# Products with 0/1 tables as two passes of high and low parts, in the forget gates and the stick-breaking attention of a two-block transformer kernel

## What is computed

```python
def stick_breaking_attention(q, k, v):           # per block of 128 queries
    z = jnp.einsum("bqhd,bshd->bhqs", qb, k) * scale
    earlier = kpos[None, :] < qpos[:, None]
    log_keep = jnp.where(earlier, jax.nn.log_sigmoid(-z), 0.0)
    log_after = lax.cumsum(log_keep, axis=3, reverse=True) - log_keep
    w = jnp.where(earlier, jnp.exp(jax.nn.log_sigmoid(z) + log_after), 0.0)
    return jnp.einsum("bhqs,bshd->bqhd", w, v)

def forgetting_attention(q, k, v, log_f):
    cum = jnp.cumsum(log_f, axis=1)
    z = jnp.einsum("bqhd,bshd->bhqs", qb, k) * scale + cq[..., None] - cum[:, :, None, :]
    p = masked_softmax(z, kpos[None, :] <= qpos[:, None])
    return jnp.einsum("bhqs,bshd->bqhd", p, v)
```

## Time and profile before

| | |
|---|---|
| median of three runs | 1865.68 us |
| the profiled execution | 1863.92 us, of it span 1861.9 us |
| TensorE products | 1841.9 us busy, 99% of the span, 9402 |
| VectorE | 1032.0 us, 55% |
| ScalarE | 876.5 us, 47% |
| GpSimd | 153.4 us, 8% |
| mean granted TensorE clock | 0.999 |

### The profile page before, as it was taken

One profiled execution on the slowest core, in us unless ns is written; L12 is line 12 of the kernel. 1 busy time (PEld: TensorE's weight loads), 2 busy tenths in 40 slices (PEclk: granted clock), 3 DMA queues, 4 the chain that ended last, 5 costly groups with the idle time before them and its releaser, 6 DMA issues.

```text
span 1861.9 us, 22247 instructions
## 1 busy us (share of the span) xinstructions
PE 1841.9 (99%) x9402; PEld 1576.7 (85%) x9402; DVE 1032.0 (55%) x997; ACT 876.5 (47%) x1076; POOL 153.4 (8%) x169
## 2 busy tenths in 40 slices
PE   8999999999999999999999999999999999999998
PEld 6889988898888998889888888888888888888886
DVE  5665544564755655447475655555455545545544
ACT  6454543564645454346363444454353444435443
POOL 1300011000240001100020000010000101100011
PEclk9999999999999999999999999999999999999999
DMA  8866555455577555545555645554546555455553
GB/s 274 239 184 205 172 169 169 128 193 192 169 215 216 168 171 192 169 137 183 192 198 187 203 159 191 180 177 166 190 156 221 178 168 180 155 165 197 181 181 113
DMA packets 187154, 338.96 MB, mean 182 GB/s; under 512 B 6848, under 2 KB 48688, under 8 KB 186160
## 3 DMA queue, kind: packets, MB, share of 16 engines
q1 hardware_dynamic: 181536, 316.89, 52.0%
q0 software_dynamic: 5232, 20.59, 4.0%
q10 hardware_dynamic: 288, 0.07, 0.0%
HBM read 335.43 MB, written 2.10 MB: 181 GB/s over the span
## 4 chain that ended last, share of the span: by engine, by line
PE 94%; DVE 2%; ACT 2%; issue 1%; DMA 0%; ACTq 0%; DVEq 0%
PE acc L1540 27%; PE acc L1542 27%; PE acc L1541 27%; PE bank L1693 3%; PE bank L1633 1%; DVE w_lo L1004 1%; PE bank L1682 1%; PE bank L1662 1%; ACT w_hi L658 1%; PE bank L1623 1%; PE bank L1801 1%; PE acc L1589 0%; PE bank L1651 0%; PE bank L1652 0%; PE bank L1650 0%
## 5 line engine op out<-in xcount | busy, mean ns | idle before, releaser
L1004 DVE TENSOR_TENSOR w_lo<-raw,w_hi 128x2048 fp32r<-128x2048 f32 (+4 forms) x308 | 675.6, 2197 | 572.9 <-ACT w_hi L658 572.7
L1540 PE MATMUL acc<-w_hi,xt_hi 128*128 128x512 f32 (+4 forms) x2400 | 909.4, 379 | 0.5 <-DVE w_lo L1004 0.3
L1542 PE MATMUL acc<-w_hi,xt_lo 128*128 128x512 f32 (+4 forms) x2400 | 902.3, 376 | 0.0
L1541 PE MATMUL acc<-w_lo,xt_hi 128*128 128x512 f32 (+4 forms) x2400 | 901.2, 376 | 0.0
L658 ACT ACTIVATE w_hi<-raw 128x2048 fp32r<-128x2048 f32 (+4 forms) x308 | 557.0, 1812 | 607.1 <-PE acc L1542 596.6
L1540 PEld LDWEIGHTS acc<-w_hi,xt_hi 128*128 128x128 f32 x2400 | 450.6, 188 | 80.0 <-issue 2.1
L1542 PEld LDWEIGHTS acc<-w_hi,xt_lo 128*128 128x128 f32 x2400 | 450.5, 188 | 79.0
L1541 PEld LDWEIGHTS acc<-w_lo,xt_hi 128*128 128x128 f32 x2400 | 450.8, 188 | 77.2 <-issue 0.5
L732 ACT ACTIVATE S<-S,nmax 128x256 f32<-128x256 f32 (+1 forms) x128 | 60.0, 470 | 38.2 <-DVE nmax L1108 21.1
L719 ACT ACTIVATE PT<-bank 128x512 f32<-128x512 f32 (+2 forms) x76 | 36.3, 556 | 72.9 <-PE bank L1682 56.7
L532 POOL DMA_DIRECT2D bias<-in_b_in x32 | 18.1, 565 | 599.2 <-DVE M L1082 208.2
(11 more groups left out here) (292 smaller groups left out, 1248.6 us busy)
## 6 DMA issues: line engine op xcount, KB each, us to landing
raw<-in_w_in SPq DMA_DIRECT2D x76, 1024.0 KB, 5.0
raw<-in_w_in_c SPq DMA_DIRECT2D x64, 1024.0 KB, 5.4
raw<-in_w_in_ab SPq DMA_DIRECT2D x52, 1024.0 KB, 5.1
raw<-in_w_out SPq DMA_DIRECT2D x32, 1024.0 KB, 5.1
raw<-in_w_out_ab SPq DMA_DIRECT2D x16, 1024.0 KB, 5.0
raw<-in_w_out_c SPq DMA_DIRECT2D x16, 1024.0 KB, 5.0
raw<-in_w_in SPq DMA_DIRECT2D x16, 688.0 KB, 4.0
raw<-in_w_in SPq DMA_DIRECT2D x16, 576.0 KB, 3.8
```

The source lines that it names most:

```text
L1004: nc.vector.tensor_tensor(lo[:, :, 0:n], raw[i % RING][:, :, 0:n], hi[:, :, 0:n].bitcast(F32), ALU.subtract).then_inc(lo_done.s, 1)
L1540: nc.tensor.matmul(s, xt_hi[:, kt, rows], hi[:, k, 0:n], start=(q == 0 and k == 0), stop=False)
L1541: nc.tensor.matmul(s, xt_hi[:, kt, rows], lo[:, k, 0:n], start=False, stop=False)
L1542: ins = nc.tensor.matmul(s, xt_lo[:, kt, rows], hi[:, k, 0:n], start=False, stop=(q == NQ - 1 and k == KQ - 1))
```

## The change

The 0/1 tables are exact in fp32r, so a product with one needs only the other operand split: data = high part (rounded to fp32r) + low part (the rest). Each product becomes two fp32r products that accumulate. GpSimd copies the three tables once into an fp32r tile `tri`, in the order le, ones, ge. In the gate stage the log gates are split on 8 values a row (`ff_hl`) and both parts are spread; the new `LB` pair takes the place of the whole of S. Neighbouring tables are read in one product (256 columns of le and ones). In the suffix sums the masked SP is split into the idle buffers of `ahead[1]`: ScalarE writes the high part, VectorE the low part, both at the end of the k = 15 list behind `transposed(l, 1, 1)`, and TensorE waits for the low part. The three blocks that used `tri_ge` are one product of 384 columns.

```diff
+        with ExitStack() as sums_over_keys:
+            LB = [sums_over_keys.enter_context(nc.sbuf_tensor(f"LB_{part}", [P, T, HB, P], F32R)) for part in ("hi", "lo")]
...
+        tri = sb("tri", [P, 3 * P], F32R)
+        ff_hl = sb("ff_hl", [P, 2, T, HB], F32R)
...
-        LB = S[:, 0:2].rearrange("p h t s -> p (h t s)").rearrange("p (t h q) -> p t h q", t=T, h=HB)
+        SPR = ahead[1]
... gpsimd, before the layers
+            nc.gpsimd.tensor_copy(tri[:, :], cst[:, CONST["tri_le"][0]:CONST["tri_le"][0] + 3 * P]).then_inc(tri_set.s, 1)
... scalar, k == 15
                     transposed(l, 1, 1)
+                    act.wait_ge(*z_masked(l, 1))
+                    nc.scalar.activation(SPR[0][:, :, 0:CAUSAL_W], SP.rearrange("p h t s -> p h (t s)")[:, :, 0:CAUSAL_W],
+                                         ACT.Copy).then_inc(soft_hi.s, 1)
... vector, k == 7
                     dve.wait_ge(*win.pt_full(l, HB))
-                    for t in range(T):
-                        ins = nc.vector.tensor_copy(LB[:, t], ff[:, 3, t, :].unsqueeze(2).broadcast_to([P, HB, HD]))
+                    nc.vector.tensor_copy(ff_hl[:, 0], ff[:, 3]).then_inc(f_hi.s, 1)
+                    dve.wait_ge(*f_hi(l, 1))
+                    nc.vector.tensor_tensor(ff_hl[:, 1], ff[:, 3], ff_hl[:, 0].bitcast(F32), ALU.subtract).then_inc(f_lo.s, 1)
+                    dve.wait_ge(*f_lo(l, 1))
+                    for part in range(2):
+                        ins = nc.vector.tensor_copy(LB[part][:, :, :, :].rearrange("p t h q -> p (t h) q"), ff_hl[:, part].rearrange(
+                            "p t h -> p (t h)").unsqueeze(2).broadcast_to([P, T * HB, P]))
... vector, k == 15
                     transposed(l, 1, 1)
+                    dve.wait_ge(*soft_hi(l, 1))
+                    nc.vector.tensor_tensor(SPR[1][:, :, 0:CAUSAL_W], SP.rearrange("p h t s -> p h (t s)")[:, :, 0:CAUSAL_W],
+                                            SPR[0][:, :, 0:CAUSAL_W].bitcast(F32), ALU.subtract).then_inc(soft_lo.s, 1)
... tensor, k == 9
                     pe.wait_ge(*f_wide(l, 1))
+                    pe.wait_ge(tri_set.s, 1)
...
-                            nc.tensor.matmul(s[:, 0:P], LB[:, 0, h, :], c("tri_le"), start=True, stop=True)
-                            nc.tensor.matmul(s[:, P:SEQ], LB[:, 0, h, :], c("ones"), start=True, stop=False)
-                            ins = nc.tensor.matmul(s[:, P:SEQ], LB[:, 1, h, :], c("tri_le"), start=False, stop=True)
+                            nc.tensor.matmul(s, LB[0][:, 0, h, :], tri[:, 0:2 * P], start=True, stop=False)
+                            nc.tensor.matmul(s, LB[1][:, 0, h, :], tri[:, 0:2 * P], start=False, stop=False)
+                            nc.tensor.matmul(s[:, P:SEQ], LB[0][:, 1, h, :], tri[:, 0:P], start=False, stop=False)
+                            ins = nc.tensor.matmul(s[:, P:SEQ], LB[1][:, 1, h, :], tri[:, 0:P], start=False, stop=True)
... tensor, k == 16
-                    pe.wait_ge(*z_masked(l, 2))
+                    pe.wait_ge(*soft_lo(l, 1))
                     for h, b in enumerate(range(4)):
                         take(b)
                         s = bank[b]
-                        first_q, last_q, last_k = (causal_part(SP, h)[:, P * n:P * n + P] for n in range(3))
-                        nc.tensor.matmul(s[:, 0:P], c("tri_ge"), first_q, start=True, stop=True)
-                        nc.tensor.matmul(s[:, P:SEQ], c("tri_ge"), last_q, start=True, stop=False)
-                        nc.tensor.matmul(s[:, P:SEQ], c("ones"), last_k, start=False, stop=True)
-                        nc.tensor.matmul(s[:, SEQ:CAUSAL_W], c("tri_ge"), last_k, start=True, stop=True).then_inc(r_full.s, 1)
+                        later, within = tri[:, P:2 * P], tri[:, 2 * P:3 * P]
+                        for part in range(2):
+                            nc.tensor.matmul(s[:, 0:CAUSAL_W], within, SPR[part][:, h, 0:CAUSAL_W], start=(part == 0), stop=False)
+                        for part in range(2):
+                            ins = nc.tensor.matmul(s[:, P:SEQ], later, SPR[part][:, h, SEQ:CAUSAL_W], start=False, stop=(part == 1))
+                        ins.then_inc(r_full.s, 1)
```

More of the change, by code:

```diff
@@ L289, in hybrid_then_banded @@
         cmp_exp, f_exp, f_ln, cmp_pt = chain("cmp_f_scalar", 1, 1, 1, 2)
-        f_biased, f_negabs, f_min, f_log, f_wide = chain("f_step", 1, 1, 1, 1, 1)
+        f_biased, f_negabs, f_min, f_log, f_hi, f_lo, f_wide = chain("f_step", 1, 1, 1, 1, 1, 1, 1)
+        tri_set = signal("tri_set", 0)
+        soft_hi, soft_lo = signal("soft_hi", 1), signal("soft_lo", 1)
         silu = dict(zip((FOX, NSA, SB, MLA), chain("silu", 1, 1, 1, 1)))
```

## The result

| | before | after |
|---|---|---|
| median of 15 runs, us | 1865.76 (1863.59 to 1868.38) | 1868.9 (1867.07 to 1874.06) |
| ratio after / before | | 1.0021, 95% interval 1.0014 to 1.0028 |
| profiled execution, us (its span) | 1863.92 (1861.9) | 1868.9 (1866.9) |
| mean granted clock of that execution | 0.999 | 0.997 |

The changed kernel is slower by 0.21% by the ratio of the runs, and by 3.1 us (0.17%) by the medians. The page of the profile says almost nothing of where they are: TensorE is still busy 99% of the span, with 0.1 us more busy time than in the earlier trace rows in a span that is 5.0 us longer, and the clock line shows only nines, because one digit stands for 47 us.

The account below looks back on a forecast made before the run. TensorE, busy 99% of the span, was taken to bound the kernel. Suffix +1.67 and gate -0.82 a layer, twice, gave +1.7 us: 1863.92 to 1865.6 for the profiled execution, median 1867.4, range 1864.9 to 1872.0.

Parts of the forecast that it names:

- Products of the gate stage: Cumulative forget gates: two 256- and two 128-column fp32r products a head, 2.68 to 1.86 us, -0.82 a layer.
- Narrow fp32r products as dear as fp32 ones: Rival, both stages: 128-column fp32r products cost 0.223 us, deciding above about 0.16; +4.5 us, 1870.2; chance 0.14.
- The gate stage that I worked out from 56 ns: Gate stage by the skill pages' figure for a 128-column pass: an estimated 1.3 us, against the forecast 1.86.
- VectorE's spreads and slot 8: Doubled spreads, 1.40 or 2.4 us, delay VectorE 1.1 to 2.1 before slot 8's last chunk; cover 2.4, cost nothing.
- The stall in front of the suffix products: Before the suffix sums TensorE waits 2.95 us for VectorE's low part; high part takes 1.48, low part 1.74.
- What sets the MLA values: After the suffix sums, VectorE's queue up to the first subtraction sets their start, before and after: +1.67 a layer.
- No stall: Rival, suffix sums: low part ready when TensorE arrives, both stages gain; -4.2 us, 1861.5; chance 0.04.
- The clock falls in the new stall: Rival, suffix stall: clock drops, up to 1.8 a layer; +4.7 us, 1870.4; chance 0.17, with dear narrow products 0.04.
- the page's line of nines: Whole kernel: the page's clock line was read as showing no fall at any place after the start.
- the median's 1.8 us over the profiled execution: Base of the forecast: median 1865.68 lies 1.8 above the profiled execution, carried along from 1865.6 to 1867.4.
- the sum that I predicted: Both stages over two layers: 2 x (1.67 - 0.82) = +1.7 us.

Follow-up runs that it names:

- the gate half alone: The change with its suffix half put back to fp32 sums, against the kernel before: 1863.94 us, ratio 0.9993.
- The full-height pair: Kernel before with compressed-attention products widened from 15 to 128 rows, 1863.5 us; the gate half on that same edit, 1861.64 us.
- The early version: Suffix half only, with ScalarE's and VectorE's passes over SP moved ahead of the second pair of transposes: 1873.42 us, ratio 1.0042.
- three versions with it and without the long wait: With 128-row compressed-attention products: kernel before, 1863.5 us; gate half, 1861.64; whole change with early suffix passes and fourth split behind the subtractions, 1860.6.
- Where the 1.01 alone was left: Early suffix passes with the fourth split moved behind the subtractions: suffix half only, 1864.78 us; whole change with 128-row compressed-attention products, 1860.6 us.

## Why the prediction was right or wrong

The prediction was 1867.4 in a range of 1864.9 to 1872.0; the time is 1868.9. By its own steps:

- *Products of the gate stage*: 1.86 us a layer predicted, 1.86 measured in the gate half alone. Its two terms were each off by 0.05 a head and cancelled: the narrow pair took 0.17 (0.06, then 0.11) where I had 2 x 0.112, and the two wide ones 0.29 (0.17, then 0.12) where I had 2 x 0.12 from the earlier trace rows; 0.46 a head against 0.464. The full-height pair gives 1861.64 - 1863.5 = -1.86 for the two layers, 0.2 more than the 1.64 that I wrote.
- *Narrow fp32r products as dear as fp32 ones*: false. 0.11 at most, where 0.16 was the point from which it would decide. The figure that I took from the Trainium skill (TensorE: Matmul & The Clock Gate, Back-to-back issue gap), an estimated 56 ns for 128 columns, fits one of the two: the trace has it for the first narrow product and twice that for the second. I had passed over the text beside that table: its 134 cycles are for an isolated product, and the same section of the Trainium skill gives about 81 ns for 128 columns in a stream of products each with its weight load; the trace's mean of the pair is 0.17 / 2 = 0.085. The gate stage that I worked out from 56 ns, 1.3 us, did not come: it was 1.86.
- *VectorE's spreads and slot 8*: cost nothing, as predicted; no wait of TensorE stands behind slot 8. The spreads took 0.69 each for 1024 elements, the lower of my two bounds.
- *The stall in front of the suffix products*: predicted 2.95, measured 2.89 from the end of the slot to the first product (2.72 in the row's own idle time). High part 1.50 against 1.48, low part 1.75 against 1.74.
- *What sets the MLA values*: VectorE's queue, not the products. Predicted +1.67 a layer, measured +1.69. The early version is the proof of the mechanism: the stall went and the 5.63 stayed.
- *No stall*, the faster rival: false in the change. That it would take VectorE's order of work to make it true is what the split moved behind the subtraction showed; but with the stall gone the MLA values came only 0.45 a layer sooner than before and not 1.29, because the third head's bank is freed late (1.01 of waiting).
- *The clock falls in the new stall*: partly true, and in part where I put it. I gave it 0.21 and up to 1.8 a layer, always in both layers. It comes in some executions and some layers, 1.2 us each time where two layers of one execution can be compared (9.61 against 8.45), as a part of it falls in time in which TensorE would wait for the subtraction, and in the profiled execution of after it did not come at all. The grounds that I set against it, dense work up to the stall, did not keep it away. The Trainium skill (TensorE: Matmul & The Clock Gate, HAM oscillation) tells of TensorE idling between groups of products. The falls behind the stall can be of that kind; those of the gate stage, with TensorE busy and no gap ahead of them, are not.
- *The missing term*: falls in the gate stage, with TensorE busy throughout. This is the step that failed. I took the page's line of nines as proof of a steady clock, and took the median's 1.8 us over the profiled execution as plain scatter to be carried along. Both readings were wrong: the 1.8 was a fall that the profiled execution of before didn't have, and the kernel after has more falls than before, 4.4 us of them in the mean of its executions against 1.7 (the balance below). Of before's executions only a third stand on the lowest step, of after's none.

The balance of means: before averages 1865.4 over its 24 executions, 1.7 above its lowest step (1863.7). The change adds 2 x (1.69 - 0.82) = 1.7, so without falls it would be at 1865.4. Its 15 executions average 1869.8, 4.4 above that. So of the 4.4 between the means 1.7 is the sum that I predicted and 2.7 is falls. (The 15 executions of before that ran beside after average 1865.8; by them it is 2.3.) The median moved by 3.1 for the same reasons; as a median of steps it is not split so neatly. A good part of after's 4.4 is falls behind the stall: with the 15-row products out of the way, the change averages 1867.75, 2.5 above the 1865.2 that would be due there. If the two kinds simply add, the rest, 1.9, comes from the gate stage, where before lost 1.7 and the gate half alone 2.4 (its mean of 1864.45 less 1862.1). So most of what the change added in falls would be the stall's. How the two kinds add up within an execution, and why one execution has a fall and the next has none, stays open.

That the forecast came near the median is then owed to a sum that was right to 0.1 us, and for the rest to luck: it stood on a base (before's median) that carried one fall unnoticed, and the falls moved the median by only 1.4 more (3.1 - 1.7). Single executions of after lie up to 6.7 above the forecast.

## What to carry to other kernels

Where TensorE is busy 99% of the span, look for what changes its clock as well as counting its products: list the single executions with their mean clock, and if they stand in steps, find the place in a window view of a few microseconds, since a page with 40 slices hides it. When a new pass goes on an engine without slack, follow its queue to the next instruction that TensorE waits for; moving the pass forward only moves the wait, and something must leave the queue. A faster instruction form on TensorE is worth its difference only where TensorE's own work ends last.

## What the hardware showed

- **TensorE's clock falls while TensorE is busy.** Behind eight fp32 products that use 15 of the 128 rows (2.05 us) the clock was at 1.2 GHz for 3.4 us (6.8 with the block cut in two), in after from 1.5 us behind the block's end, in none, one or both layers of an execution. The same block with 128 rows takes 1.95 us, and the 11, 10 and 7 executions of three versions with it and without the long wait kept to one step. Such a fall cost 1.6 us in the rows, near the steps of 1.5 to 2.1 us between executions.
- **A wait of 2.72 us can have a fall behind it.** Behind it the clock fell 1.0 us later for 3.4 us in one layer and not in the other, at a price of 1.2 us. The version whose wait was split in 1.01 and 1.96 was no better off (1873.42, all five executions at 0.997 or less, a fall in one of the two layers of the profiled one). Where the 1.01 alone was left, no fall followed in either layer of two profiled executions; with waits of 0.37 and 1.38 (the low part on GpSimd) one of 6.8 us followed in both layers. So the length of the longest wait alone doesn't tell them apart.
- **GpSimd is no free engine beside VectorE's subtractions.** One subtraction of 1536 elements takes it 3.52 us where VectorE takes 1.75, and it cost VectorE's queue nearly as much (1.63) as it took off it.
- **fp32r at 128 columns** stands 0.06 and 0.11 us from its neighbour, an fp32 product 0.22; so a narrow one costs a half or less. A spread of 1024 elements into fp32r takes VectorE 0.69, where two of 512 into fp32 took 0.70 together:

```profile
179.46 0.69 DVE L1241 CAST LB_hi<-ff_hl 128x1024 fp32r<-128x1024 f32 x1
```
